# Stage ends of a two-block network on one core: residual sums in pairs, an early norm sum, one rounding pass, and an eight-slot ring for the query weights

## The chip, the core and the metric

The kernel runs on one core of a Trainium2 chip. The metric is the device time of one execution in microseconds, smaller is better. TensorE (PE in the profile) multiplies, VectorE (DVE), ScalarE (ACT) and GpSimd (POOL) do elementwise work, and DMA queues issued by SyncE (SP) and POOL bring weights from memory. All engines run their own instruction streams in order and meet in semaphores.

## The reference

One activation x of 256 tokens by 1024 features goes through ten sublayers, each of the same frame: normalise, mix, add to x.

```
h = modulate(x, norm_g, shift, scale)      # rms_norm over the 1024 features, then scale and shift
x = x + gate[:, None, :] * sublayer(h)     # (0.5 * gate for the four swiglu sublayers)
```

The sublayers in order: swiglu (0), the bidirectional SSD mixer (1), swiglu (2), swiglu (3), latent attention, MLA (4), swiglu (5), then twice an RWKV and pooling mixer (6, 8) followed by PEER (7, 9), and a last rmsnorm. PEER is

```
q = (h @ peer_q).reshape(B, S, PEER_HEADS, 2, PEER_HALF)
scores = jnp.einsum('bshpd,hpkd->bshpk', q, peer_keys)     # then top 16 of each half, and of the sums
act = jax.nn.gelu(jnp.einsum('td,ted->te', hx, u_sel), approximate=False)
return jnp.einsum('te,ted->td', gx * act, v_sel)
```

and the kernel computes it densely over all 128 x 128 experts. At the end of SSD, y is normalised in groups and projected: `rms_norm(y) @ w_out`. Everything is float32.

## The kernel before

x lies in SBUF feature-major, as eight tiles `x[:, d, :]` of 128 features by 256 tokens. Every weight matrix is cut into blocks of 128 x 1024 float32 (512 KB), and all of them stand in one `stream` in the order of use; SP issues them one after the other, each as soon as the block before it in its slot was used (semaphore `block_used`). `ring_plan` gives each block a slot: RING = 4 slots proper, and in some stages up to eight more in a large scratch tile (`arena`; MORE). CYCLES says which slots a stage goes round.

A float32 product is made from three fast products. ACT rounds a block to its high part (`split_hi`, L1126, into one of four buffers `weights_hi`, so block n waits for block n-4), DVE subtracts and leaves the low part in the slot (`split_lo`, L1613), and PE does hi x hi, hi x lo and lo x hi: 24 matmuls for a block (L506 where the output is a column of tiles, L539 where a block adds to all eight tiles of `acc`). The output projections of the RWKV mixers (L996) use plain float32.

The frame around every stage is written by hand on four engines:

- DVE, `residual`: x[:, d] += acc[:, d] * gate for d = 0..7 (L1607), each signalled with `x_upd`. Ahead of it DVE makes the low parts of the next stage's first two blocks.
- ACT, `norm_squares`: eight squares (L1109), then Sqrt and Identity of their sum (L1111, L1112). Ahead of it ACT makes the high parts of the next stage's first two or three blocks.
- PE, `norm_sum`: eight float32 matmuls with a matrix of ones (L487, 16 records in the trace).
- DVE, `normed`: reciprocal (L1587), three refinement steps (L1534 to L1536), then h (L1592); ACT adds the shift (L1118); PE starts the next stage at L518. Between its sum and L518 PE runs 16 matmuls on zeros (`open_acc`, L493), once the low parts of the first two blocks are there.

In stages 0, 2, 3, 5 (swiglu, "row blocks") and 7, 9 (PEER) the last weights are row blocks: each adds to all eight tiles of acc, so all tiles are finished by the last block. In the mixers 1, 4, 6, 8 each output block finishes one tile ("column blocks"): SSD has 16 output blocks in two passes, MLA and RWKV eight.

In MLA, POOL issues four loads in one queue once stage 3 has updated x (L2173 to L2176): the positions, w_uq, w_ukv and a table. DVE starts the angles of the rotary embedding (L1751 to L1761) when the positions have landed, ahead of the low parts of blocks 4, 5, 6 of the stage. At the end of SSD, DVE normalises y tile by tile (L1733), ACT rounds it (L1244) and DVE takes the rest (L1728); the splits of output blocks 4 to 7 stand between these tiles. In PEER, ACT copies query k out of PSUM (L1445) and then splits block k+4, and PE makes the scores (L1040).

## Time and profile before

| | |
|---|---|
| median of 3 runs | 3544.99 us (3544.09 to 3548.17) |
| the profiled execution, its own time | 3544.45 us |
| its span, first to last instruction | 3542.7 us |
| PE busy | 3363.8 us, 95% |
| DVE, ACT, POOL busy | 73%, 1609.1 us, 6% |
| mean granted TensorE clock | 0.982 |

The profile is of one execution. "Idle before" is the time an engine had nothing to do ahead of an instruction; what stands behind the arrow is what ended that time. A busy PE also contains the 16 zero matmuls at each stage's start, and time at half clock.

### The profile page before, as it was taken

The page shows a single profiled execution, that of the slowest core. Times are in us where ns is not written, and L with a number is a line of the kernel's source. Part 1 is how long each engine was busy: PE and PEld are TensorE (multiplying, and loading weights), DVE is VectorE, ACT ScalarE, POOL GpSimd, SP SyncE. Part 2 cuts the span into 40 slices and gives each one's busy share as a digit, 9 for nine tenths or more (in the row PEclk, how much of TensorE's full clock was granted, in tenths as well). Part 3 has the DMA queues.
Part 4 walks back from the last instruction along what each step waited for, and adds up shares of the span by engine and source line. Part 5 has one row for each costly group of instructions (what it writes and reads, how often), then busy time and mean ns, then how long its engine had stood idle before and what let it go on. Part 6 is the DMA issues. An engine that isn't in the chain of part 4 may idle for free.

```text
span 3542.7 us, 68786 instructions
## 1 busy us (share of the span) xinstructions
PE 3363.8 (95%) x26804; PEld 3227.9 (91%) x26804; DVE 2582.7 (73%) x4576; ACT 1609.1 (45%) x2583; POOL 198.8 (6%) x331
## 2 busy tenths in 40 slices
PE   6999989999999998999999989999899999999998
PEld 5999869999867998889999989998789999989998
DVE  7879667788736886746977757776845978767776
ACT  3456644354445435234454444444414444444444
POOL 1100001101000220200000000000300000000000
PEclk9999999999999999999999999999999999999999
DMA  9954218869622993035664466665214665456665
GB/s 366 358 196 170 78 48 326 311 254 335 215 78 107 394 354 125 31 105 190 233 205 168 164 203 228 227 227 173 72 57 158 232 222 173 166 180 228 229 227 174
DMA packets 246577, 707.44 MB, mean 200 GB/s; under 512 B 27472, under 2 KB 93008, under 8 KB 244928
## 3 DMA queue, kind: packets, MB, share of 16 engines
q1 hardware_dynamic: 212112, 571.64, 46.3%
q0 software_dynamic: 34224, 132.46, 10.0%
q8 instruction: 166, 2.72, 0.3%
q14 instruction: 75, 0.61, 0.1%
HBM read 669.40 MB, written 34.60 MB: 199 GB/s over the span
## 4 chain that ended last, share of the span: by engine, by line
PE 83%; DVE 7%; DMA 5%; ACT 3%; issue 2%; SPq 0%; ACTq 0%; DVEq 0%; POOLq 0%; POOL 0%
PE psum L506 37%; PE psum L539 27%; PE psum L1061 3%; DMA ring<-stream 3%; PE psum L883 2%; PE psum L996 1%; PE psum L634 1%; DMA arena<-mod_weights 1%; DVE ring L1613 1%; PE psum L903 1%; DVE arena L1544 1%; PE psum L518 1%; PE psum L519 1%; ACT weights_hi L1126 1%; DVE arena L1670 1%
## 5 line engine op out<-in xcount | busy, mean ns | idle before, releaser
L1126 ACT ACTIVATE weights_hi<-ring 128x1024 fp32r<-128x1024 f32 x727 | 769.0, 1058 | 1068.3 <-DMA ring<-stream 1017.7
L1613 DVE TENSOR_TENSOR ring<-ring,weights_hi 128x1024 fp32r<-128x1024 f32 x727 | 890.0, 1226 | 477.6 <-ACT weights_hi L1126 474.5
L506 PE MATMUL psum<-hh,weights_hi 128*128 128x256 f32 x4216 | 1210.6, 287 | 20.0 <-ACT arena L1339 8.5
L506 PE MATMUL psum<-h,weights_hi 128*128 128x256 f32 x4216 | 1196.6, 284 | 0.0
L506 PE MATMUL psum<-hh,ring 128*128 128x256 f32 x3104 | 881.5, 284 | 0.0
L506 PEld LDWEIGHTS psum<-hh,weights_hi 128*128 128x128 f32 x4216 | 813.1, 193 | 27.0 <-issue 11.9
L539 PE MATMUL psum<-small,weights_hi 128*128 128x256 f32 x2752 | 783.4, 285 | 39.9 <-DVE work L1648 21.6
L506 PEld LDWEIGHTS psum<-h,weights_hi 128*128 128x128 f32 x4216 | 812.9, 193 | 0.2
L539 PE MATMUL psum<-work,weights_hi 128*128 128x256 f32 x2752 | 781.6, 284 | 0.0
L539 PE MATMUL psum<-small,ring 128*128 128x256 f32 x2304 | 651.3, 283 | 0.0
L506 PEld LDWEIGHTS psum<-hh,ring 128*128 128x128 f32 x3104 | 598.0, 193 | 0.0
L539 PEld LDWEIGHTS psum<-small,weights_hi 128*128 128x128 f32 x2752 | 523.7, 190 | 42.0 <-issue 22.7
L539 PEld LDWEIGHTS psum<-work,weights_hi 128*128 128x128 f32 x2752 | 524.1, 190 | 0.0
L539 PEld LDWEIGHTS psum<-small,ring 128*128 128x128 f32 x2304 | 438.0, 190 | 0.0
L506 PE MATMUL psum<-hh,more_lo 128*128 128x256 f32 x1112 | 315.3, 284 | 0.0
L1544 DVE SCALAR_TENSOR_TENSOR arena<-arena 128x1024 f32<-128x1024 f32 x232 | 281.7, 1219 | 9.7 <-DMA arena<-mod_weights 9.6
L1613 DVE TENSOR_TENSOR more_lo<-arena,weights_hi 128x1024 fp32r<-128x1024 f32 x198 | 241.5, 1223 | 60.2 <-ACT weights_hi L1126 60.1
L1126 ACT ACTIVATE weights_hi<-arena 128x1024 fp32r<-128x1024 f32 x198 | 208.2, 1053 | 113.6 <-PE psum L506 86.2
L506 PEld LDWEIGHTS psum<-hh,more_lo 128*128 128x128 f32 x1112 | 214.1, 193 | 0.0
L2072 DVE TENSOR_SCALAR work<-kept,small 128x128 f32<-128x128 f32 x512 | 142.7, 342 | 82.6 <-PE psum L1061 77.3
L2084 DVE TENSOR_TENSOR work<-work,arena 128x256 f32<-128x256 f32 x256 | 159.5, 625 | 5.4 <-PE psum L539 5.4
L2154 POOL DMA_DIRECT2D arena<-mod_weights x208 | 109.8, 528 | 600.5 <-DVE arena L1544 597.0
(409 smaller groups left out, 3904.7 us busy)
## 6 DMA issues: line engine op xcount, KB each, us to landing
ring<-stream SPq DMA_DIRECT2D x751, 512.0 KB, 3.5
arena<-mod_weights POOLq DMA_DIRECT2D x224, 512.0 KB, 5.9
arena<-stream SPq DMA_DIRECT2D x206, 512.0 KB, 5.5
acts<-small SPq DMA_DIRECT2D x256, 128.0 KB, 2.2
work<-acts SPq DMA_DIRECT2D x256, 128.0 KB, 2.1
arena<-cond_rows POOLq DMA_DIRECT2D x3, 1024.0 KB, 9.0
arena<-w_uq POOLq DMA_DIRECT2D x1, 3072.0 KB, 10.4
arena<-constants POOLq DMA_DIRECT2D x2, 1200.0 KB, 5.7
```

What stands on the lines that cost most here:

```text
L506: mm = pe.matmul(out, lhs[:, d, :], rhs[:, d, :], start=(d == 0 and p == 0), stop=(d == DT - 1 and p == 2))
L518: pe.matmul(out, w[:, d, :], h_hi[:, d, :], start=opens and d == 0, stop=False, skip_group_check=True)
L519: pe.matmul(out, wl[:, d, :], h_hi[:, d, :], start=False, stop=False, skip_group_check=True)
L539: mm = pe.matmul(acc[:, d, :], lhs[:, d, :], rhs, start=False, stop=False, skip_group_check=True)
L883: mm = pe.matmul(PS[:, (4 * st + b) % 8, j * P:(j + 1) * P], lhs[:, c, :], rhs[:, c, :], start=True, stop=True)
L1061: mm = pe.matmul(PS[:, 4 + g % 4, j * P:(j + 1) * P], OHI[:, g % 2, j, :], OHJ[:, g % 2, j, :], start=True, stop=True)
L1126: act.activation(whi[:, NTH[n] % WS, :], raw(n), ACT.Copy).then_inc(sem["block_hi"], 1)
L1544: return dve.scalar_tensor_tensor(PRODUCT[:, m % 2, :], block, 1.0, COND[:, 0 if g < 6 else 1, :], ALU.mult, ALU.mult, accum_out=modc[:, g ...
L1613: dve.tensor_tensor(low(n), raw(n), whi[:, NTH[n] % WS, :].bitcast(F32), ALU.subtract)\
L2072: dve.tensor_scalar(OHI[:, g % 2, j, :], iota, ijg[:, 0, t:t + 1], ijg[:, 2, t:t + 1], ALU.is_equal, ALU.mult)
L2084: dve.tensor_tensor(gat[:, k % 4, :], sil[:, k % 4, :], WALL[:, :, i * 4 + k], ALU.mult).then_inc(sem["pe_gated"], 1)
L2154: pool.dma_start(MODRING[slot], mods[i * MOD_RING + (first + slot + MOD_RING)]).then_inc(mod_full[slot], 16)
```

## The change

1. **Row-block ends** (stages 0, 2, 3, 5, 7, 9). PE signals `acc_done` in the last block when tiles 0-1, 2-3 and 4-5 are finished, and `residual` waits for those instead of for the whole block. PEER's loop over value blocks gets its last round written out for that.
2. **Mixer ends** (1, 4, 6, 8). `residual` of a pair of tiles runs as soon as their blocks are through, placed between the low-part splits; the splits of the next stage's first two blocks now stand behind tiles 0-5 and behind tiles 6-7, on ACT and on DVE. PE sums the squares of tiles 0-3 ahead of the last output block and those of 4-7 behind it.
3. **Root table.** ACT runs a one-column Sqrt at each stage end ahead of the squares.
4. **SSD.** All 16 tiles of y are rounded first, then blocks 4 to 15 are split.
5. **Query ring.** PEER's 16 query blocks go round eight slots, four of them in the arena, which is free once x was updated (`ARENA_FREE`).
6. `acc_done` takes the place of the semaphore `mla_pos`: the positions now count on `mla_w` with the other three loads, and DVE waits for all four.

```
 CYCLES = {...
-          BASE["mix_in", 0]: (0, range(RING))}
+          BASE["mix_in", 0]: (0, range(RING)), **{BASE["peer_q", l]: (0, query_cycle(l)) for l in range(2)},
+          **{BASE["uv", l]: (query_cycle(l)[0], range(RING)) for l in range(2)}}
-ARENA_FREE = {BASE["ffn", f] + RING - 1: 8 * s for f, s in ((1, 2), (3, 5))}
+ARENA_FREE = {**{BASE["ffn", f] + RING - 1: 8 * s for f, s in ((1, 2), (3, 5))},
+              **{BASE["peer_q", l] + RING: 8 * (7 + 2 * l) for l in range(2)}}
+def query_cycle(l):
+    first = (BASE["peer_q", l] - BASE["mix_in", 0]) % RING
+    return (*((first + k) % RING for k in range(RING)), *SSD_CYCLE[RING:])
+BEHIND_MIXERS = (2, 5, 7, 9)
+BY_ROWS = (0, 2, 3, 5, 7, 9)
...
-            def rows_in_parts(w, wl, hi, lo):
+            def rows_in_parts(w, wl, hi, lo, last=False):
                 for d in range(DT):
                     ...
+                    if last and d in (1, 3, 5):
+                        mm.then_inc(sem["acc_done"], 1)
...
+                        if b == 1 and d == 6:
+                            norm_sum(2, 0, 4)
...
-                pe.wait_ge(sem["mla_w"], 48)
+                pe.wait_ge(sem["mla_w"], 64)
...
+                    if d == 6:
+                        norm_sum(7 + 2 * l, 0, 4)
...
-                norm_sum(s)
+                norm_sum(s, 4 if s in BEHIND_MIXERS else 0)
...
                     act.activation(YHI[:, k, :], Y[:, k, :], ACT.Copy).then_inc(sem["ssd_yhi"], 1)
-                    if k in (8, 10, 12, 14):
-                        split_hi(o0 + k // 2)
-                for n in range(8, 2 * DT):
+                for n in range(4, 2 * DT):
                     split_hi(o0 + n)
...
             for s in range(NSUB):
-                if s and s in IN_PARTS:
-                    for p in range(3 if s in EARLY else 2):
+                act.activation(eps[:, 6 + s:7 + s], eps[:, 0:1], ACT.Sqrt)
+                if s in BEHIND_MIXERS:
+                    norm_squares(s, 0, 6)
+                    split_hi(FIRST[s])
+                    norm_squares(s, 6, DT)
+                    split_hi(FIRST[s] + 1)
+                else:
+                    for p in range(0 if s == 0 else 3 if s in EARLY else 2):
                         split_hi(FIRST[s] + p)
-                norm_squares(s)
+                    norm_squares(s, 0, DT)
+                norm_root(s)
...
+            def residual(s, last, a=0, b=DT):
+                for d in range(a, b):
+                    if s in BY_ROWS and d < 6:
+                        dve.wait_ge(sem["acc_done"], 3 * BY_ROWS.index(s) + d // 2 + 1)
+                    else:
+                        ready(last(d | 1))
+                    dve.scalar_tensor_tensor(x[:, d, :], acc[:, d, :], modc[:, s, 16 + d:17 + d], x[:, d, :], ALU.mult, ALU.add)\
+                       .then_inc(sem["x_upd"], 1)
+            def residual_by_columns(s, last, a):
+                residual(s, last, a, 6)
+                split_lo(FIRST[s + 1])
+                residual(s, last, 6, DT)
+                split_lo(FIRST[s + 1] + 1)
...
-                dve.wait_ge(sem["mla_pos"], 16)
+                dve.wait_ge(sem["mla_w"], 64)
...
-            pool.dma_start(ANG[:, 0, :].bitcast(I32), pos_d[0:1, :].to_broadcast([64, T])).then_inc(sem["mla_pos"], 16)
+            pool.dma_start(ANG[:, 0, :].bitcast(I32), pos_d[0:1, :].to_broadcast([64, T])).then_inc(sem["mla_w"], 16)
```

Three places of the instruction streams are shown as they stand in the program. The first is ACT at the end of SSD, where `weights_hi` is a split, `arena<-x` are the squares and `small<-psum,eps` is the root. Before:

```order
L1126 ACTIVATE weights_hi<-ring 128x1024 [waits block_used,slot_full_0]
L1126 ACTIVATE weights_hi<-ring 128x1024 [waits block_used,slot_full_1]
L1126 ACTIVATE weights_hi<-ring 128x1024 [waits block_used,slot_full_2]
L1109 ACTIVATE arena<-x 128x256 [waits x_upd] x8
L1111 ACTIVATE small<-psum,eps 128x256 [waits norm_sum]
```

Now:

```order
L1155 ACTIVATE weights_hi<-ring 128x1024 [waits block_used,slot_full_0]
L1520 ACTIVATE eps<-eps 128x1
L1136 ACTIVATE arena<-x 128x256 [waits x_upd] x6
L1155 ACTIVATE weights_hi<-ring 128x1024 [waits block_used,slot_full_1]
L1136 ACTIVATE arena<-x 128x256 [waits x_upd] x2
L1155 ACTIVATE weights_hi<-ring 128x1024 [waits block_used,slot_full_2]
L1140 ACTIVATE small<-psum,eps 128x256 [waits norm_sum]
```

The second split of the next stage has moved from ahead of all squares to behind the last of them, ahead of the root. The second place is DVE at the end of the first RWKV mixer, where `x<-psum,modc,x` is the residual, `ring<-ring,weights_hi` a low part, and RECIPROCAL opens the norm. Before:

```order
L1960 TENSOR_TENSOR arena<-arena 128x1024 [waits rw_bg,dve_chain]
L1613 TENSOR_TENSOR ring<-ring,weights_hi 128x1024 [waits block_hi] x2
L1607 SCALAR_TENSOR_TENSOR x<-psum,modc,x 128x256 [waits block_used] x8
L1587 RECIPROCAL small<-small 128x256 [waits norm_sqrt]
L1534 SCALAR_TENSOR_TENSOR arena<-small 128x256 [waits norm_sqrt,dve_chain]
```

Now:

```order
L2010 TENSOR_TENSOR arena<-arena 128x1024 [waits rw_bg,dve_chain]
L1642 SCALAR_TENSOR_TENSOR x<-psum,modc,x 128x256 [waits block_used] x6
L1661 TENSOR_TENSOR ring<-ring,weights_hi 128x1024 [waits block_hi]
L1642 SCALAR_TENSOR_TENSOR x<-psum,modc,x 128x256 [waits block_used] x2
L1661 TENSOR_TENSOR ring<-ring,weights_hi 128x1024 [waits block_hi]
L1623 RECIPROCAL small<-small 128x256 [waits norm_sqrt]
```

Six residuals have moved ahead of both low parts, and one low part now stands between the last residual and the reciprocal. The third is PE at the same mixer end (`arena,kept` is the norm sum, `arena,ring` an output block). Before:

```order
L996 MATMUL psum<-arena,ring 128x256 [waits slot_full_0]
L996 MATMUL psum<-arena,ring 128x256 x3
L996 MATMUL psum<-arena,ring 128x256 [waits slot_full_1]
L996 MATMUL psum<-arena,ring 128x256 x3
L996 MATMUL psum<-arena,ring 128x256 [waits slot_full_1]
L996 MATMUL psum<-arena,ring 128x256 x3
L487 MATMUL psum<-arena,kept 128x256 [waits norm_sq] x8
L493 MATMUL psum<-zeros 128x512 [waits block_lo]
```

Now:

```order
L1015 MATMUL psum<-arena,ring 128x256 x3
L499 MATMUL psum<-arena,kept 128x256 [waits norm_sq] x4
L1015 MATMUL psum<-arena,ring 128x256 [waits slot_full_1]
L1015 MATMUL psum<-arena,ring 128x256 x3
L1015 MATMUL psum<-arena,ring 128x256 [waits slot_full_1]
L1015 MATMUL psum<-arena,ring 128x256 x3
L499 MATMUL psum<-arena,kept 128x256 [waits norm_sq] x4
L506 MATMUL psum<-zeros 128x512 [waits block_lo]
```

Four of the eight sum matmuls have moved ahead of the last output block.

## Rows read from the trace of the kernel before

**Rows 1.** The page, busy time, share of the span and instructions of each engine.

```profile
PE 3363.8 (95%) x26804; PEld 3227.9 (91%) x26804; DVE 2582.7 (73%) x4576; ACT 1609.1 (45%) x2583; POOL 198.8 (6%) x331
```

**Rows 2.** Timeline of PE, first swiglu's end: start us, us, engine, line, tiles, count, idle.

```profile
242.93 3.72 PE L487 MATMUL psum<-arena,kept 128*128 128x256 f32 x16 [1.02 <-ACT arena L1109]
...
251.68 0.39 PE L518 MATMUL psum<-hh,weights_hi 128*128 128x256 f32 x1 [1.58 <-ACT hh L1118]
```

**Rows 3.** Timeline of ACT at the same place.

```profile
236.19 0.42 ACT L1148 ACTIVATE small<-arena 128x256 fp32r<-128x256 f32 x1 [2.46 <-PE psum L539]
236.51 2.00 ACT L1126 ACTIVATE weights_hi<-ring 128x1024 fp32r<-128x1024 f32 x2
239.13 1.06 ACT L1126 ACTIVATE weights_hi<-ring 128x1024 fp32r<-128x1024 f32 x1 [0.62 <-PE psum L539]
242.46 3.16 ACT L1109 ACTIVATE arena<-x 128x256 f32<-128x256 f32 x8 [2.27 <-DVE x L1607]
245.64 1.28 ACT L1111 ACT_TABLE_LOAD   x1
```

**Rows 4.** Timeline of DVE at the same place.

```profile
237.59 2.36 DVE L1613 TENSOR_TENSOR ring<-ring,weights_hi 128x1024 fp32r<-128x1024 f32 x2 [0.52 <-ACT weights_hi L1126]
241.94 3.23 DVE L1607 SCALAR_TENSOR_TENSOR x<-psum,modc,x 128x256 f32<-128x256 f32 x8 [1.99 <-PE psum L539]
...
247.44 1.75 DVE L1587 RECIPROCAL small<-small 128x256 f32<-128x256 f32 x1 [1.14 <-ACT small L1111]
```

**Rows 5.** Line L1238, a one-column Sqrt: duration min/median/max ns.

```profile
L1238 ACT ACTIVATE eps<-eps x1: 202/202/202, 486.9 to 486.9; 128x1 f32<-128x1 f32 x1
```

**Rows 6.** Timeline of PE, end of the first RWKV mixer.

```profile
1534.69 24.44 PE L996 MATMUL psum<-arena,ring 128*128 128x256 f32 x112
1558.96 3.62 PE L487 MATMUL psum<-arena,kept 128*128 128x256 f32 x16
```

**Rows 7.** Timeline of DVE at the same place.

```profile
1563.12 1.75 DVE L1587 RECIPROCAL small<-small 128x256 f32<-128x256 f32 x1 [2.16 <-ACT small L1111]
```

**Rows 8.** Timeline of PE at the end of SSD.

```profile
550.70 0.28 PE L682 MATMUL psum<-more_lo,ring 128*128 128x256 f32 x1
```

**Rows 9.** Timeline of DVE at the end of SSD.

```profile
555.98 1.75 DVE L1587 RECIPROCAL small<-small 128x256 f32<-128x256 f32 x1 [2.03 <-ACT small L1111]
```

**Rows 10.** Waits of PE from 505 to 530 us: total, times, longest.

```profile
PE psum L682 <- DVE ring L1613: 4.1, 4, 2.2
```

**Rows 11.** Line L2176, issue of the last of the four MLA loads at 968.4.

```profile
DMA to landing us min/median/max: 15.4/15.4/15.4
```

**Rows 12.** Timeline of DVE in the MLA input.

```profile
979.59 0.29 DVE L1751 CAST arena<-arena 64x256 f32<-64x256 int32 x1
...
983.75 0.29 DVE L1761 TENSOR_SCALAR arena<-arena 64x256 f32<-64x256 f32 x1
986.63 1.23 DVE L1613 TENSOR_TENSOR ring<-ring,weights_hi 128x1024 fp32r<-128x1024 f32 x1 [2.59 <-ACT weights_hi L1126]
```

**Rows 13.** Timeline of PE, block 4 of the MLA input.

```profile
987.91 0.39 PE L506 MATMUL psum<-hh,weights_hi 128*128 128x256 f32 x1 [3.06 <-DVE ring L1613]
```

**Rows 14.** Timeline of PE in the queries and scores of both PEER stages.

```profile
1580.47 0.38 PE L506 MATMUL psum<-hh,weights_hi 128*128 128x256 f32 x1 [1.33 <-DVE ring L1613]
...
1616.91 7.30 PE L1040 MATMUL psum<-arena 128*128 128x128 f32 x63 [1.63 <-ACT arena L1445]
...
2671.97 0.39 PE L506 MATMUL psum<-hh,weights_hi 128*128 128x256 f32 x1 [0.82 <-DVE ring L1613]
...
2709.60 8.81 PE L1040 MATMUL psum<-arena 128*128 128x128 f32 x62 [2.82 <-ACT arena L1445]
```

**Rows 15.** Windows: length, busy time (count) of PE, PEld, DVE, ACT, POOL; clock, DMA, GB/s.

```profile
405.00:420.00 15.00, 9.21 (x50) 6.46 (x49) 4.10 (x4) 9.23 (x21) 0.00 (x0) 0.77 0.09 35
411.00:416.60 5.60, 5.06 (x21) 3.53 (x22) 1.90 (x3) 5.30 (x13) 0.00 (x0) 0.50 0.00 0
898.40:901.30 2.90, 2.87 (x13) 2.90 (x14) 0.22 (x1) 0.00 (x0) 0.53 (x1) 0.50 0.89 329
988.00:991.40 3.40, 3.40 (x29) 3.40 (x30) 2.47 (x3) 3.40 (x8) 0.00 (x0) 1.00 0.05 18
2709.60:2713.80 4.20, 4.20 (x23) 4.20 (x24) 0.93 (x1) 2.14 (x3) 0.00 (x0) 0.59 0.01 6
```

**Rows 16.** Timeline of PE where a long wait of a swiglu stage ends.

```profile
898.43 0.55 PE L539 MATMUL psum<-small,weights_hi 128*128 128x256 f32 x1 [4.25 <-DVE work L1648]
```

More of the change, by code:

```diff
@@ L290, in build @@
         zeros = sb("zeros", [P, P], BF16)
-        eps = sb("eps", [P, 6])
+        eps = sb("eps", [P, 20])
         modc = sb("modc", [P, NSUB, 24])
@@ L482, in arrived, with norm_sum @@
                 return raw(n).rearrange("p (k c) -> p k c", k=8)
-            def norm_sum(s):
-                for d in range(DT):
+            def norm_sum(s, a=0, b=DT):
+                for d in range(a, b):
                     pe.wait_ge(sem["norm_sq"], 8 * s + d + 1)
-                    mm = pe.matmul(PS[:, 2, 0:T], ones, SQ[:, d, :], start=(d == 0), stop=(d == DT - 1))
-                mm.then_inc(sem["norm_sum"], 1)
+                    mm = pe.matmul(PS[:, 2, 0:T], ones, SQ[:, d, :], start=(d == 0), stop=(d == DT - 1), skip_group_check=True)
+                if b == DT:
+                    mm.then_inc(sem["norm_sum"], 1)
             def open_acc():
@@ L1065, in peer, with value @@
                 open_acc()
-                with pe.Fori(0, NK // 4) as i:
+                def value(k, i, last=False):
+                    w, wl = parts(v0 + k, i)
+                    pe.wait_ge(sem["gate_lo"], i * 4 + (GATES["uv", l] + k + 1))
+                    rows_in_parts(w, wl, gat_hi[:, k, :], gat_lo[:, k, :], last)
+                with pe.Fori(0, NK // 4 - 1) as i:
                     for k in range(4):
-                        w, wl = parts(v0 + k, i)
-                        pe.wait_ge(sem["gate_lo"], i * 4 + (GATES["uv", l] + k + 1))
-                        rows_in_parts(w, wl, gat_hi[:, k, :], gat_lo[:, k, :])
+                        value(k, i)
+                for k in range(4):
+                    value(k, NK // 4 - 1, k == 3)
             def begin(s):
-                norm_sum(s)
+                norm_sum(s, 4 if s in BEHIND_MIXERS else 0)
             pe.wait_ge(sem["inits"], 4)
@@ L1103, in ready, with norm_squares @@
                 act.wait_ge(sem["block_used"], i * STEP + (n + 1))
-            def norm_squares(s):
-                for d in range(DT):
+            def norm_squares(s, a, b):
+                for d in range(a, b):
                     if s:
@@ L1510, in _ @@
                     peer((s - 7) // 2)
-            norm_squares(NSUB)
+            act.activation(eps[:, 6 + NSUB:7 + NSUB], eps[:, 0:1], ACT.Sqrt)
+            norm_squares(NSUB, 0, DT)
+            norm_root(NSUB)
         @block.vector
@@ L1598, in normed, with residual_by_rows @@
                     split_lo(FIRST[s] + 3)
-            def residual(s, last):
+            def residual(s, last, a=0, b=DT):
+                for d in range(a, b):
+                    if s in BY_ROWS and d < 6:
[4 more added lines that the diff above has]
+                       .then_inc(sem["x_upd"], 1)
+            def residual_by_rows(s, last):
                 if s + 1 in FIRST:
@@ L1604, in residual @@
                         split_lo(FIRST[s + 1] + p)
-                for d in range(DT):
-                    ready(last(d | 1))
-                    dve.scalar_tensor_tensor(x[:, d, :], acc[:, d, :], modc[:, s, 16 + d:17 + d], x[:, d, :], ALU.mult, ALU.add)\
-                       .then_inc(sem["x_upd"], 1)
+                residual(s, last)
+            def residual_by_columns(s, last, a):
[3 more added lines that the diff above has]
+                split_lo(FIRST[s + 1] + 1)
             def split_lo(n, i=0):
@@ L1657, in ffn @@
                     products(2 * FT + j)
-                residual(s, lambda d: base + 3 * FT - 1)
+                residual_by_rows(s, lambda d: base + 3 * FT - 1)
             def ssd():
@@ L1736, in ssd @@
                         rest_of_y(k - 1)
-                    if k in (8, 10, 12, 14):
-                        split_lo(o0 + k // 2)
                 rest_of_y(ZT - 1)
-                for n in range(8, 2 * DT):
+                for n in range(4, 2 * DT):
                     split_lo(o0 + n)
-                residual(1, lambda d: BASE["ssd_out"] + DT + d)
+                    if n in (13, 15):
+                        residual(1, lambda d: o0 + DT + d, n - 13, n - 11)
+                residual_by_columns(1, lambda d: o0 + DT + d, 4)
             def mla():
-                dve.wait_ge(sem["mla_pos"], 16)
+                dve.wait_ge(sem["mla_w"], 64)
                 c1, c2 = 6.28125, 1.93500518798828125e-3
@@ L1822, in mla @@
                     split_lo(o0 + n)
-                residual(4, lambda d: o0 + d)
+                    if n in (5, 7):
+                        residual(4, lambda d: o0 + d, n - 5, n - 3)
+                residual_by_columns(4, lambda d: o0 + d, 4)
             def rwkv(l):
@@ L2104, in peer @@
                     gate_lo(k + 2, NK // 4 - 1)
-                residual(7 + 2 * l, lambda d: BASE["uv", l] + 2 * NK - 1)
+                residual_by_rows(7 + 2 * l, lambda d: BASE["uv", l] + 2 * NK - 1)
             dve.wait_ge(sem["inits"], 4)
```

9 lines of the change are left out of this document (6 added, 3 removed).

## The prediction

> **What bounds the kernel now.** The page's row of busy times comes first: PE is busy 95% of the span, and the next engine, DVE, 73% [rows 1]. So an edit pays only where it shortens an idle time of PE or a stretch at half clock; what it takes off ACT or DVE elsewhere is worth nothing. Then the timelines of one stage end. In stage 0 the last matmul ends at E = 242.93 - 1.02 = 241.91. From there the chain runs: DVE's residuals from 241.94 (eight in 3.23, 0.40 each) [rows 4], ACT's squares from 242.46, PE's sum from 242.93 for 3.72 (it starts on the first squares and ends behind the last), a table load at 245.64 for 1.28 [rows 2, 3], the root, the reciprocal at 247.44 [rows 4], and the next stage's first matmul at 251.68 [rows 2]. That is 5.5 us from E to the reciprocal, and 4.24 from there, which the change leaves alone. The 16 zero matmuls lie in this second part, so PE looks busy in a time that is chain. Outside the ends the change touches three places where PE waits: output blocks of SSD [rows 10], block 4 of MLA [rows 13], and queries and scores of PEER [rows 14].
>
> **A. Row-block ends (minus 4.4).** The last elementwise step of the stage on ACT ends at 236.61, 5.3 ahead of E, and the splits for the next stage follow [rows 3]. Now a root table load (1.28, rows as above) and a one-column Sqrt (0.20 [rows 5]) stand between: the pair of splits (2.00) begins near E - 3.8, and DVE's pair of low parts (2.36, begun 1.1 behind the splits [rows 4]) ends near E - 0.4. The residuals can start there and not earlier, although tiles 0-1 are finished 18 matmuls before E: the splits, not PE, now set their start. Before, it was E + 0.03, so 0.48 is won. Behind the squares the load of 1.28 vanishes, but ACT's last square ended at 245.62 while PE's sum ended at 246.65; the root waited for the later of load (246.92) and sum. Without the load it waits for the sum: 0.24 won. Together 0.7 for stages 0, 2 and 5. In 3 ACT's splits wait for blocks to land and I take 0.6; in 7 both splits and low parts are late for that cause, 0.2. At stage 9 no splits follow, so residuals start as their tiles finish; the reciprocal then lies as at the RWKV end, where residuals already run during the last blocks: 1563.12 - 1559.13 = 3.99 behind E [rows 6, 7], against 5.5: 1.5. Sum 3 x 0.7 + 0.6 + 0.2 + 1.5 = 4.4. Bounds: 2 if the splits slip by what ACT now has in front of them; 9 if at each end the reciprocal came at 3.99.
>
> **B. Mixer ends (plus 2.6).** Half of PE's sum is moved ahead of the last output block: eight records of 3.62/16 = 0.226 [rows 6], taken as 1.72 for their pitch of 0.215. PE has nothing to wait for there (112 matmuls in 24.44 without a gap [rows 6]), so nothing hides it: the stage's last matmul moves to E' = E + 1.72. What follows E' is shorter: residuals of tiles 6 and 7 (0.87), their squares to E' + 1.4, then the high part of block F + 1 (1.06 [rows 3]) before the root on ACT, and the low part of F + 1 (1.23 [rows 12]) before the reciprocal on DVE, which comes at E' + 3.5 = E + 5.2. SSD had it at 555.98 - 550.98 = 5.00 [rows 8, 9]: plus 0.2. MLA's end, with its table load, I take as unchanged. The RWKV ends had 3.99: plus 1.2 each. Sum 2.6. Bounds: 0 if PE's early sum falls into a pause that the new order makes; 4 x 1.72 = 6.9 if the part behind E' is not shortened at all. Queued behind the low part of F + 1 are the reciprocal on DVE and the zero matmuls on PE, which begin near E' + 3.6 and take 3.6, ending about half a microsecond ahead of the first matmul's input: costed at nothing on that cover; a later low part would be paid in full.
>
> **C. SSD (minus 1.9).** PE waits four times, 4.1 in all, longest 2.2 [rows 10]. The longest is output block 4 landing, before any split, and stays. The other three, 1.9 together, fall where splits stand between roundings of y; all roundings are ahead now. Bounds: 0 (DVE's rest of y is the slow partner) to 1.9.
>
> **D. MLA's positions (plus 4.3).** The angles took DVE from 979.59 to 984.04, 4.45, as soon as the positions were there; then DVE idled 2.59 and made the low part of block 4 at 986.63 [rows 12]; PE began the block at 987.91 after a wait of 3.06 [rows 13]. Now DVE waits for all four loads. The last was issued at 968.4 and landed 15.4 later [rows 11]: 983.8, or some 0.3 earlier as stage 3 ends earlier. The angles then end near 988.05, the low part near 989.3, and PE starts at 989.4, where it could have started at 987.3 (part A): plus 2.0, with the idle time at 5.1. Queued behind the wait on DVE are the low parts of blocks 4, 5 and 6, and PE waits for them. The second cost is the clock. After the wait of 3.06 here the granted clock was 1.00; after 4.25 elsewhere [rows 16] the next 2.90 us ran at 0.50; in 405 to 420, where PE idled 5.8 in all, 5.60 us behind the restart ran at 0.50 (1.2 GHz of 2.4) [rows 15]. Half of such a stretch is lost, 1.45 to 2.8; a wait of 5.1 lies nearer to the longer one, and I take 2.3. Sum 4.3, bounds 0 (the loads land earlier) to 2.0 + 2.8 + 0.6 = 5.4.
>
> The Trainium skill (TensorE: Matmul & The Clock Gate, section "HAM oscillation") counts the loss as half of the whole throttled duration, the part under idle time included. The row from 405 to 420 has a clock of 0.77, so 6.9 us of it throttled, and by the page 3.4 would be lost where my reading of the row gives 2.8; the forecast by the page would be 1.1 higher, 3538.9. The row speaks for the smaller: part of the throttled time lay where PE had no work.
>
> **E. Query ring (minus 7.3).** Blocks 4 to 7 no longer wait for a slot. Stage 7: the wait of 1.33 goes. The 1.63 before the scores came from ACT, which had to split a late block before it copied the last query; without that, what stays is the copy and two handovers, some 0.48: 1.15 won. Stage 9: 0.82 goes, 2.82 becomes 0.48 (2.34) [rows 14], and with it the slow stretch behind: 4.20 at clock 0.59 [rows 15]; the scores took 8.81 for 62, at stage 7's rate of 7.30/63 it would be 7.18 [rows 14]: 1.6. Sum 2.5 + 4.8 = 7.3. Bounds: 2.6 if only the ring's own waits and a little of the others go (the keys and the new blocks share the queues), 7.9 if the score waits vanish whole. The arena slots open with the mixer's last residual, some 15 us before they are used.
>
> At nothing I cost the peeled loop round, 10 more signals, and the table load at stage 0's start (hidden: there DVE's products set the pace). If that cover were gone, 1.3 for the table.
>
> **Sum.** -4.4 + 2.6 - 1.9 + 4.3 - 7.3 = -6.7; from the profiled execution's own 3544.45 that is 3537.8. The median is 0.5 above this execution. About 0.2%, 7.1 us, is what a measurement of this kernel can tell from no change, so the forecast stands on that border.
>
> **Rivals.** (1) *MLA costs nothing*: the last load lands early enough, or the clock holds as it did after 3.06. Then -6.7 - 2.3 = -9.0 at least, 3535.4. Against it, 15.4 is a measured landing. (2) *The mixer ends lose the clock*: behind E' PE has only residual time, then four sums, then nothing till the low part of F + 1, 1.6 and 0.5 us idle, and a wait of 2.82 was enough for 0.59 [rows 14, 15] while 3.06 was not [rows 13]. If each of four ends lost the most that rows show, 2.8 or 2.9, that is 11.6: 3549.4, slower than before; it decides from 1.7 an end. Against it: the first part before E' is dense work. (3) *Landing bounds the queries*: part E gives only 2.6, 3542.5, no change. For it: weights come at 329 GB/s in a loaded stretch [rows 15], and the eight slots ask for more at once. (4) *The early signals work fully*: residuals start before the splits matter and the mixer sum is hidden; A gives 9 and B 0: -6.7 - 4.6 - 2.6 = -13.9, 3530.5.
>
> **How the numbers follow.** Forecast 0.48 (its own range 3534.5 to 3541), rival 1 0.15, rival 2 0.08, rival 3 0.13, rival 4 0.13, the rest 0.03. The range runs from 3531.0, which leaves out half of rival 4 and what is below, to 3545.0, which leaves out rival 2 and the rest. Faster by over 0.2% means under 3537.9: half of the forecast, rival 1 and most of rival 4, 0.50. Slower needs 3552.1: half of rival 2 and a bit, 0.05. The rest, 0.45, is no change that shows.
>
> **What the new profile would show.** A: reciprocal at E + 4.8 at stage 0, with the low parts ending just before the first residual, and E + 4.0 at the last end. B: sum records in two lots of eight; in the RWKV mixers the reciprocal 3.5 behind the last matmul, and that matmul 1.7 later. C: one PE wait left in the output blocks of SSD. D: an idle time near 5 ahead of MLA's block 4, and a clock of 0.5 behind it. E: no wait at query block 4, about 0.5 ahead of the scores, and 7.2 to 7.4 for the second scores. The forecast fails if the landing of MLA's loads has moved, if the low part of F + 1 delays the reciprocal, or if the ten ends drop the clock anywhere new.

## The result and the profile after

The changed kernel takes 3525.15 us, the median of 5 runs (3516.6 to 3529.28), against 3544.2 for the kernel before on the same chip (3543.79 to 3548.17). The ratio is 0.9941, with an interval of 0.9927 to 0.9956: 19 us less, where 6.7 were forecast and 3531.0 was the low end of the range. The busy times hardly differ from [rows 1]; here from the page of the changed kernel:

```profile
PE 3352.7 (95%) x26804; PEld 3213.5 (91%) x26804; DVE 2582.6 (73%) x4576; ACT 1610.4 (46%) x2594; POOL 199.4 (6%) x331
```

PE does the same 26,804 matmuls in 11.1 us less busy time. A shorter wait does not shorten busy time, so most of the gain is no wait at all. First the places that the prediction named.

The end of stage 0 in the changed kernel, timelines of PE, ACT and DVE (start, duration, engine, line):

```profile
239.85 3.72 PE L499 MATMUL psum<-arena,kept 128*128 128x256 f32 x16 [0.51 <-ACT arena L1136]
...
248.36 0.39 PE L531 MATMUL psum<-hh,weights_hi 128*128 128x256 f32 x1 [1.33 <-ACT hh L1147]
```

```profile
234.11 1.28 ACT L1520 ACT_TABLE_LOAD   x1
235.41 0.20 ACT L1520 ACTIVATE eps<-eps 128x1 f32<-128x1 f32 x1
235.52 2.94 ACT L1155 ACTIVATE weights_hi<-ring 128x1024 fp32r<-128x1024 f32 x3
```

```profile
236.59 2.36 DVE L1661 TENSOR_TENSOR ring<-ring,weights_hi 128x1024 fp32r<-128x1024 f32 x2 [2.04 <-ACT weights_hi L1155]
238.87 3.22 DVE L1642 SCALAR_TENSOR_TENSOR x<-psum,modc,x 128x256 f32<-128x256 f32 x8
...
244.11 1.75 DVE L1623 RECIPROCAL small<-small 128x256 f32<-128x256 f32 x1 [0.89 <-ACT small L1140]
```

E is 239.85 - 0.51 = 239.34. (E is the end of the stage's last matmul, as in the prediction.) The splits wait behind the table load, the residuals start 0.47 ahead of E, right behind the low parts, and the reciprocal comes 4.77 behind E instead of 5.53 [rows 2, 4]. The end of the first RWKV mixer, PE and then DVE:

```profile
1553.37 1.89 PE L499 MATMUL psum<-arena,kept 128*128 128x256 f32 x8
1555.10 3.62 PE L1015 MATMUL psum<-arena,ring 128*128 128x256 f32 x16
```

```profile
1561.06 1.23 DVE L1661 TENSOR_TENSOR ring<-ring,weights_hi 128x1024 fp32r<-128x1024 f32 x1 [1.43 <-ACT weights_hi L1155]
1562.20 1.75 DVE L1623 RECIPROCAL small<-small 128x256 f32<-128x256 f32 x1
```

Eight sum records stand ahead of the last block (1553.37 to 1555.10, 1.73), and the reciprocal comes 1562.20 - 1558.72 = 3.48 behind the last matmul, right behind the low part. The MLA input, DVE, PE, and the window behind PE's restart (length, busy time, count for PE, PEld, DVE, ACT, POOL, then clock):

```profile
976.63 0.29 DVE L1799 CAST arena<-arena 64x256 f32<-64x256 int32 x1 [4.88 <-DMA arena<-constants]
```

```profile
982.40 0.58 PE L519 MATMUL psum<-hh,weights_hi 128*128 128x256 f32 x1 [5.36 <-DVE ring L1661]
```

```profile
981.00:987.90 6.90, 5.50 (x26) 5.50 (x27) 4.72 (x5) 2.68 (x5) 0.00 (x0) 0.51 0.01 3
```

DVE now waits for the last load (arena<-constants), PE idles 5.36, and the next 5.5 us run at half clock, 2.7 us lost. Last the waits of PE in SSD's output blocks and from the second PEER's start to its scores (total, times, longest), and these scores:

```profile
PE psum L697 <- DVE ring L1661: 2.2, 1, 2.2
```

```profile
PE psum L1061 <- ACT arena L1472: 0.5, 1, 0.5
PE psum L531 <- ACT hh L1147: 0.4, 1, 0.4
```

```profile
2699.22 7.41 PE L1061 MATMUL psum<-arena 128*128 128x128 f32 x64 [0.47 <-ACT arena L1472]
```

One wait is left in SSD, none at the query blocks, 0.47 ahead of the scores, and these run at full pace.

So the steps of the forecast stand in the trace. What is new lies where PE waits for nothing. The windows below are of PE alone: 70 to 160 lies in the column blocks of stage 0, 3200 to 3400 in the row blocks of the second PEER; columns are length, busy time (count of matmuls), clock, DMA share, GB/s. Before:

```profile
70.00:160.00 90.00, 90.00 (x752) 1.00 0.97 365
3200.00:3400.00 200.00, 200.00 (x1669) 1.00 0.68 228
```

and after:

```profile
70.00:160.00 90.00, 90.00 (x752) 1.00 0.97 365
3200.00:3400.00 200.00, 200.00 (x1699) 1.00 0.70 232
```

PE is busy all the time at full clock in all four, yet fits 30 more row-block matmuls into the same 200 us. Taken over the whole trace, as the mean time from the recorded start of one matmul to the next of the same line (distances of 100 to 130 ns, which leaves waits and half clock out; this time is called the pace below), column blocks (L506, now L519) stay at 119.92 and 119.93 ns, and row blocks (L539, now L552) go from 119.99 to 118.35. With some 8,100 such distances that is 13.3 us, all four swiglu stages and both PEER stages having a part. Within one trace the row blocks change among 117.3, 118.7 and 120.0 from stretch to stretch.

### The profile page after: what moved, and what is told of

It is laid out like the page before. It is cut to its first block, busy times and chain, and to the rows that moved or that the text cites. A ratio compares the mean times of both kernels' runs of the same rounds, so it can differ in the third digit from the quotient of the medians.

```text
span 3523.1 us, 68787 instructions
## 1 busy us (share of the span) xinstructions
PE 3352.7 (95%) x26804; PEld 3213.5 (91%) x26804; DVE 2582.6 (73%) x4576; ACT 1610.4 (46%) x2594; POOL 199.4 (6%) x331
## 4 chain that ended last, share of the span: by engine, by line
PE 83%; DVE 7%; DMA 5%; ACT 2%; issue 2%; SPq 0%; POOL 0%; DVEq 0%; POOLq 0%; ACTq 0%
PE psum L519 37%; PE psum L552 26%; PE psum L1082 3%; DMA ring<-stream 2%; DMA arena<-mod_weights 2%; PE psum L902 2%; PE psum L1015 1%; PE psum L649 1%; DVE ring L1661 1%; DVE arena L1580 1%; PE psum L922 1%; PE psum L697 1%; PE psum L531 1%; ACT weights_hi L1155 1%; PE psum L532 1%
## 5 line engine op out<-in xcount | busy, mean ns | idle before, releaser
L519 PE MATMUL psum<-hh,weights_hi 128*128 128x256 f32 x4216 | 1210.7, 287 | 21.0 <-ACT arena L1366 8.4
L519 PE MATMUL psum<-h,weights_hi 128*128 128x256 f32 x4216 | 1195.8, 284 | 0.0
L1155 ACT ACTIVATE weights_hi<-ring 128x1024 fp32r<-128x1024 f32 x711 | 751.9, 1058 | 955.5 <-DMA ring<-stream 899.7
L1661 DVE TENSOR_TENSOR ring<-ring,weights_hi 128x1024 fp32r<-128x1024 f32 x711 | 870.2, 1226 | 412.1 <-ACT weights_hi L1155 407.1
L519 PE MATMUL psum<-hh,ring 128*128 128x256 f32 x2976 | 843.9, 284 | 0.0
L519 PEld LDWEIGHTS psum<-hh,weights_hi 128*128 128x128 f32 x4216 | 812.7, 193 | 27.8 <-issue 12.4
L552 PE MATMUL psum<-small,weights_hi 128*128 128x256 f32 x2752 | 780.4, 284 | 40.3 <-DVE work L1696 22.9
L519 PEld LDWEIGHTS psum<-h,weights_hi 128*128 128x128 f32 x4216 | 812.7, 193 | 0.3
L552 PE MATMUL psum<-work,weights_hi 128*128 128x256 f32 x2752 | 778.1, 283 | 0.0
L552 PE MATMUL psum<-small,ring 128*128 128x256 f32 x2304 | 649.5, 282 | 0.0
L519 PEld LDWEIGHTS psum<-hh,ring 128*128 128x128 f32 x2976 | 573.2, 193 | 0.0
L552 PEld LDWEIGHTS psum<-small,weights_hi 128*128 128x128 f32 x2752 | 525.2, 191 | 43.3 <-issue 23.9
L552 PEld LDWEIGHTS psum<-work,weights_hi 128*128 128x128 f32 x2752 | 525.3, 191 | 0.0
L552 PEld LDWEIGHTS psum<-small,ring 128*128 128x128 f32 x2304 | 438.0, 190 | 0.0
L519 PE MATMUL psum<-hh,more_lo 128*128 128x256 f32 x1240 | 351.6, 284 | 0.0
L1661 DVE TENSOR_TENSOR more_lo<-arena,weights_hi 128x1024 fp32r<-128x1024 f32 x214 | 261.1, 1223 | 76.8 <-ACT weights_hi L1155 73.7
L1155 ACT ACTIVATE weights_hi<-arena 128x1024 fp32r<-128x1024 f32 x214 | 225.0, 1053 | 114.1 <-PE psum L519 87.0
L519 PEld LDWEIGHTS psum<-hh,more_lo 128*128 128x128 f32 x1240 | 238.7, 192 | 0.0
```

The lines of the kernel that those rows point to most:

```text
L519: mm = pe.matmul(out, lhs[:, d, :], rhs[:, d, :], start=(d == 0 and p == 0), stop=(d == DT - 1 and p == 2))
L552: mm = pe.matmul(acc[:, d, :], lhs[:, d, :], rhs, start=False, stop=False, skip_group_check=True)
L1155: act.activation(whi[:, NTH[n] % WS, :], raw(n), ACT.Copy).then_inc(sem["block_hi"], 1)
L1661: dve.tensor_tensor(low(n), raw(n), whi[:, NTH[n] % WS, :].bitcast(F32), ALU.subtract)\
```

## What the diff holds beside the parts

## Experiments

**e1, e2: the place alone, and everything but the place.** The first is the kernel before with one edit:

```
-        eps = sb("eps", [P, 6])
+        eps = sb("eps", [P, 20])
```

> The kernel before with one edit: the tile eps has 20 columns and not 6, as the change made it, so that work and small, declared behind it, lie 64 bytes higher. In the changed kernel the summands of my prediction came out nearly as forecast (about 7 us), and some 12 us more were won in stretches where PE never waits: the matmuls of the row blocks follow each other every 117.3 to 118.7 ns, before every 120.0; those of the column blocks stay at 120.0. Theory P (place): the moving operands of the row blocks (in small and work) lie elsewhere, and that sets the pace. Then this kernel alone gains 8 to 14 us, 3530 to 3536, and its row blocks run at 117.3 to 118.7 ns. Rival C (code): the pace comes from the instructions that the change adds or from the peeled loop; then 3544, no difference, 120.0 ns.

Measured: 3532.23 against 3547.92, ratio 0.9955 (0.9940 to 0.9969). Row blocks 118.28 ns, column blocks 119.94. The row-block window:

```profile
3200.00:3400.00 200.00, 200.00 (x1685) 1.00 0.71 230
```

The second is the changed kernel with the old addresses:

```
-        eps = sb("eps", [P, 20])
+        sb("room", [P, 6])
...
         small, (gat_hi, _) = sb_twice("small", ...)
+        eps = sb("eps", [P, 20])
```

> The changed kernel, but eps is declared behind small and a tile of 6 columns stands in its old place, so that work and small lie at the addresses that they had before. Theory P: the row blocks go back to 120.0 ns, and the time is what my forecast's steps alone give, 3536 to 3538. Rival C: as the changed kernel, 3525, with 117.3 to 118.7 ns.

Measured: 3537.37 (3535.94 to 3545.64), ratio 0.9966 (0.9953 to 0.9979). Row blocks 119.99 ns. The reciprocals stand as in the changed kernel, 4.72 behind E at stage 0 and 3.49 and 3.48 at the mixers; only at stage 7 does it come later, 5.97 behind E instead of 5.08. Both edits answer for the place, and the rival is out: the code without the new place has the old pace, the new place without the code the new one. As a number the time is what the forecast's steps gave (3537.8), but that comes of another chip; its distance to the 3547.9 of before on that chip, 7.5 to 16.7 by the interval, is somewhat more than 6.7. Both kernels spread over some 10 us there, so e2's total is no finer test than that.

**e3: the query ring alone** (part 5 of the diff put into the kernel before).

> The kernel before with the query ring alone (part E). Forecast of that part: minus 7.3 against before, 3537: waits of 1.33 and 0.82 at query block 4 gone, the waits ahead of the scores 0.5 instead of 1.6 and 2.8, and no half clock in the second scores. Rival: the new blocks compete with the keys for the queues, minus 2.6.

Measured: 3541.99, ratio 0.9981 (0.9972 to 0.9990), 3.5 to 9.9 us less. From the first matmul of the stage to the end of its experts, stage 7 is 1.7 shorter and stage 9 5.4, 7.1 together against 7.3; up to the end of the scores, where the step was priced, it is 2.7 and 5.0. PE's waits in 2655 to 2730, where [rows 14] had 0.82 and 2.82:

```profile
PE psum L528 <- ACT hh L1128: 1.3, 1, 1.3
PE psum L1050 <- ACT arena L1455: 0.5, 1, 0.5
```

**e4: MLA's positions waited for alone.**

```
-                dve.wait_ge(sem["mla_w"], 64)
+                dve.wait_ge(sem["aux_loads"], 32)
...
-            ... to_broadcast([64, T])).then_inc(sem["mla_w"], 16)
+            ... to_broadcast([64, T])).then_inc(sem["aux_loads"], 16)
```

> The changed kernel, but the positions count on a semaphore of their own (the one of an early load), and DVE waits for them alone, as before (part D undone). Forecast of that part: 4.3 less than the changed kernel, 3521, the wait ahead of block 4 of MLA near 3 us and no half clock behind it. Rival: the clock does not follow the wait, 2.0 less; or the loads are not late, no difference. The pace of the row blocks varies from run to run in the changed kernel (3516.6 to 3529.3), so the difference is to be read in the MLA stage of the profile.

Measured: 3523.99 (3519.81 to 3528.8), ratio 0.9927 (0.9914 to 0.9939). PE's wait ahead of block 4, and the clock behind it:

```profile
981.13 0.39 PE L519 MATMUL psum<-hh,weights_hi 128*128 128x256 f32 x1 [3.27 <-DVE ring L1661]
```

```profile
981.60:985.00 3.40, 3.40 (x19) 0.50 0.02 6
```

The wait is back at 3.3, but against the expectation the clock fell here too, for 3.4 us (1.7 lost), which it had not after 3.06 in [rows 13, 15]. From the first matmul of MLA to its last the three traces have 159.7 (before), 166.1 (changed) and 163.1 (e4). Of the 6.4 between the first two 1.7 is the early sum, so the positions cost 4.7 against the trace of before, and 3.0 against e4, whose clock happened to fall.

**e5 to e8: four other places.** To e4's kernel, whose tiles lie as in the changed one: unused tiles ahead of h and ahead of modc, with eps declared last:

```
+        sb("room_h", [P, 8])      # 8, 16, 24, 32: h and hh 32, 64, 96, 128 bytes up
         h, (h_lo,) = sb_twice("h", ...)
...
-        eps = sb("eps", [P, 20])
+        sb("room", [P, 8])        # 8, 16, 16, 16: small and work 32, 96, 128, 160 bytes up
```

> The last run had moved nothing; here, in the changed kernel with its own wait for positions, unused tiles are put ahead of h and work, and eps is declared last. Addresses modulo 128: h and hh (moving operands of the column blocks) 32, before 0; small and work (of the row blocks) 0; they were 96 in the kernel before (pace 120.0 ns) and 32 in the changed one (117.3 to 118.7). Theory M (the start modulo 128 decides): the column blocks take over the pace 117.3 to 118.7 that the row blocks had at 32, and win 1 to 2% of some 1500 us, 15 to 28 us; the row blocks at 0 go back to 120.0, as the column blocks had at 0, and lose 12. Together 3507 to 3525. Rival R (where the moving operand lies relative to weights_hi, ring and the results decides): no rule by 128, paces other than these.

> As the run before, with h, hh, small and work all at 64 modulo 128. Theory M: rows and columns have one pace, whichever it is; if only 32 is good, both 120.0 ns and 3534 to 3538. Rival R: two paces.

> As the run before, all at 96 modulo 128, where the row blocks of the kernel before stood (128 bytes below). Theory M: both at 120.0 ns, 3534 to 3538. Rival R: the rows differ from 120.0 although the remainder is the same.

> As the run before, with h and hh 128 bytes above their old place, so at 0 modulo 128 as before; small and work at 0. Theory M: both at 120.0 ns, 3534 to 3538, the columns as before because the remainder is the same. Rival R: a pace other than 120.0 in the column blocks, since the absolute place is new.

Measured: 3504.24 (ratio 0.9873, 0.9854 to 0.9891), 3475.49 (0.9793, 0.9777 to 0.9809), 3524.89 (0.9931, 0.9915 to 0.9948) and 3528.11 (0.9939, 0.9922 to 0.9955). The windows of e6:

```profile
70.00:160.00 90.00, 90.00 (x766) 1.00 0.98 373
3200.00:3400.00 200.00, 199.43 (x1704) 1.00 0.72 232
```

The column blocks can be moved to a better pace too, and they are the larger family. Theory M fell: at 96 modulo 128 the rows had 119.99 before and 118.32 in e7, and rows and columns at 64 have two paces, 115.34 and 117.38. The guess that only 32 is good gave 3534 to 3538 for e6; it was the best of the four.

**e9, e10: everything moved, or hh without h.** An unused tile of 64 bytes ahead of ring (e9) or between h and hh (e10), in the kernel before.

> The kernel before with one edit: an unused tile of 64 bytes ahead of ring, so that every tile, weights and moving operands alike, lies 64 bytes higher. So far the mean distance of two matmuls was, with h at +0, 32, 64, 96, 128 bytes: 119.92, 116.86, 117.38, 119.92, 119.05 ns; with small and work at +0, 32, 64, 96, 128, 160: 119.99, 118.95, 118.35, 115.34, 118.32, 119.98. The remainder by 128 alone does not give these, but 32 and 64 are the fast ones. Theory D (distance between the moving operand and the weights decides, the two being read side by side): both paces stay at 119.9 and 120.0 ns and the time at that of before. Rival A (the absolute address decides): columns 117.4, rows 118.4, and 30 to 50 us less than before.

> The kernel before with an unused tile of 64 bytes between h and hh: the low part h stays where it was, the high part hh and what lies behind (small and work too) are 64 bytes higher. hh is read by two of three matmuls of a column block, h by one. If each moving operand acts by itself, the columns get two thirds of the gain at +64, from 119.9 to some 118.2 ns; if both must be in the same place, they stay at 119.9 or become slower. Rows 118.4 as in the changed kernel at +64.

Measured: e9 3550.13, ratio 1.0006 (0.9995 to 1.0017), 119.91 and 119.98 ns; e10 3530.38, ratio 0.9951 (0.9935 to 0.9968), columns 118.90, rows 118.10. The stage 0 window of e9 has the old count:

```profile
70.00:160.00 90.00, 90.00 (x753) 1.00 0.97 365
```

Absolute addresses are out. In e10 columns won 1.0 ns, against 2.5 with both parts moved: less than the two thirds expected, and more than nothing. The single steps show more. The two of three that start with a matmul on hh take 117.3 ns in the mean, the pace of a column block at +64, and the one that starts with h takes 122.0, more than the 119.9 that it had before. So each operand shows its own place, and h beside a moved hh is worse off than both in the old place.

**e11, e12: the norm sum whole, and another pair of places.** e11 is e6 without `norm_sum(s, 0, 4)` ahead of the last output blocks; e12 is e6 with h at +32.

```
-                    if d == 6:
-                        norm_sum(7 + 2 * l, 0, 4)
...
-                norm_sum(s, 4 if s in BEHIND_MIXERS else 0)
+                norm_sum(s)
```

> The layout of e6 (h and work at 64 modulo 128) with a part of the change undone: PE makes the whole norm sum behind the last output block of the four mixers (DVE and ACT keep the new order). By part B of the prediction the early half costs 1.72 us of PE and is not won back: the last matmul comes 1.7 earlier and the reciprocal 4.0 behind it instead of 3.5, so 1.2 less at each of four ends, 4.8 less than e6. Rival: without the early half the sum cannot start before the squares of tiles 6 and 7, and the reciprocal comes 5.2 behind the last matmul, no difference.

> Each family at its best place so far: h and hh at +32 bytes (116.86 ns), small and work at +96 (115.34 ns). If a family's pace hangs on its own place alone, the columns are 0.5 ns faster than in e6, 12,200 x 0.5 = 6 us less than e6. Rival: the small difference between +32 and +64 is one of runs, not of place, and the time equals e6's within 5 us.

Measured: e11 3479.54 (ratio 0.9803, 0.9787 to 0.9819), e12 3486.98 (0.9831, 0.9809 to 0.9853), columns 117.58 and 117.06 ns, rows 116.22 and 115.64. The reciprocal of e11 comes 4.00 behind the last matmul at all four mixers, as forecast, but the paces differ from run to run by more than 4.8 us makes. e12 was expected 6 below e6 and won nothing on it, by ratio either (0.9831 against 0.9793).

**e13, e14: what the distance is taken from, and its period.** In the kernel before, an unused tile of 64 bytes behind weights_hi (e13), or of 256 bytes ahead of h (e14).

> The kernel before with an unused tile of 64 bytes behind weights_hi: ring and weights_hi keep their place, everything else (arena, x, h, hh, small, work) lies 64 bytes higher, the distances among it unchanged. Theory W (what counts is the distance from the moving operand to the weights that are loaded beside it): columns near 117.4 ns as in e6, rows near 118.1 to 118.4 as in the changed kernel and e10; blocks whose low part lies in the arena, moved along, gain less. About 40 us less than before. Rival O (distance to other tiles, where the other engines and DMA work): 119.9 and 120.0 ns, no difference.

> The kernel before with an unused tile of 256 bytes ahead of h, so that h, hh, small and work lie 256 bytes higher. By +128 the columns went from 119.92 to 119.05 ns and the rows from 119.99 to 118.32. If the pace repeats every 256 bytes: 119.9 and 120.0 ns, no difference. Rival: it doesn't, and the paces come out like those at +128, 10 to 20 us less.

Measured: e13 3512.22, ratio 0.9904 (0.9887 to 0.9920), by it 34 us less, where about 40 were expected; columns 117.30 ns, rows 118.45. e14 3550.28, ratio 1.0006 (0.9995 to 1.0017), 119.92 and 119.99. Their windows of stage 0, e13 first:

```profile
70.00:160.00 90.00, 90.00 (x776) 1.00 0.99 379
```

```profile
70.00:160.00 90.00, 90.00 (x753) 1.00 0.99 367
```

e13 and e9 differ only in whether ring and weights_hi moved along. The output blocks of SSD and MLA, whose moving operands lie in the arena, went from 119.8 to 120.0 in the other traces to 117.5 and 117.8 in this one. So the distance to ring and weights_hi counts, and 256 bytes more change nothing. ACT, DVE and the DMA write these two as well, a rival to the weights that PE reads there. It does not fit: the column steps of e13 take 117.31 ns with DVE busy and 117.25 without, 117.36 and 117.24 with ACT busy and not, 117.24 and 117.58 with more than two DMA packets under way and fewer; in the trace before all six lie at 119.9 to 120.0. Sorted by the distance from weights_hi to the moving operand modulo 256, one remainder gives nearly one mean in all traces so far, within 0.6 ns, and within 0.9 for the rows at 192 (worked out as above):

```
remainder  mean distance of matmuls, ns
   0       columns 119.92 (before), 119.91 (e9), 119.92 (e14); rows 119.98 (e8)
  32       columns 116.86 (e5), 117.06 (e12)
  64       columns 117.38 (e6), 117.58 (e11), 117.30 (e13)
  96       rows 119.99 (before, e2, e3, e14), 119.98 (e9); columns 119.92 (e7)
 128       rows 118.95 (e5); columns 119.05 (e8)
 160       rows 118.35 (changed), 118.28 (e1), 118.64 (e4), 118.45 (e13), 118.10 (e10)
 192       rows 115.34 (e6), 116.22 (e11), 115.64 (e12)
 224       rows 118.32 (e7)
```

**e15, e16: a place that the curve names.** Columns had not been at 192; `room_h` and `room` get 48 columns each.

> The changed kernel with its own wait for positions; h and hh 192 bytes above their old place, small and work at 192 modulo 256 from weights_hi as in e6. Theory W256 (the remainder of the distance by 256 decides, for both families): columns 115.3 to 116.2 ns, as the rows had there, against 117.4 in e6; 12,200 x 1.2 to 2.1 = 15 to 25 us less than e6, 3450 to 3462. Rival: the rows' 115.3 belongs to the row blocks, and the columns stay above 117.

> As e15, with PE's norm sum whole behind the last output block of the four mixers, as in e11. By part B 4.8 us less than e15, the last matmul of a mixer 1.7 earlier and the reciprocal 4.0 behind it instead of 3.5. e11 against e6 showed 4.0 and 3.49 in the profile, but the two times could not be told apart.

Measured: e15 3455.80 (3454.34 to 3459.72), ratio 0.9731 (0.9718 to 0.9745); columns 114.04 ns, rows 116.18. e16 3456.22 (3446.04 to 3464.9), ratio 0.9739 (0.9725 to 0.9752); 113.81 and 115.25. The page of e15 and its two windows:

```profile
PE 3270.5 (95%) x26804; PEld 3125.1 (90%) x26804; DVE 2583.7 (75%) x4576; ACT 1609.0 (47%) x2594; POOL 196.6 (6%) x331
```

```profile
70.00:160.00 90.00, 90.00 (x767) 1.00 0.98 370
3200.00:3400.00 200.00, 199.72 (x1718) 1.00 0.73 235
```

The time fell into the range that the rule gave (3450 to 3462), but the columns, expected at 115.3 to 116.2, were faster than the rows at that place. The window of stage 0 in e16, which has the same layout:

```profile
70.00:160.00 90.00, 90.00 (x797) 1.00 1.01 390
```

The same blocks at the same place make 767 matmuls in one trace and 797 in the other. Taken block by block, the means above are mixtures. At remainders 64 and 192 alike a block runs either at some 113.4 ns or at some 117.8 and at nothing between, and the remainders differ in how often: of the column blocks 5 to 11% are at the fast level at 64 (e6, e11, e13) and 87 to 91% at 192 (e15, e16), of the row blocks 36 to 58% at 192 (e6, e11, e12, e15, e16). No trace has a block at the fast level at another remainder.

The end of the first RWKV mixer in e16, PE and DVE:

```profile
1519.38 3.62 PE L501 MATMUL psum<-arena,kept 128*128 128x256 f32 x16
```

```profile
1523.54 1.75 DVE L1619 RECIPROCAL small<-small 128x256 f32<-128x256 f32 x1 [0.43 <-ACT small L1136]
```

That is 4.00 behind E = 1519.54, and without the 1.73 ahead of it. The two medians do not show the 4.8 us; only the stage end in the profile does.

## Why the prediction was wrong

The step that failed is the sentence on what is costed at nothing. It names the peeled loop, the signals and a table load, and not the wider eps, and the whole sum takes the pace of a dense matmul as given. The tile was read as storage; what it moved was worth 13.3 us in the trace (8,100 x 1.64 ns), twice all the forecast's steps, and 16 (11 to 21) by the ratio of e1, which has that edit alone. No rival had that mechanism, so the range ended 6 us too early.

The steps themselves, each with its size from the traces:

- **A** (4.4 forecast): the way from E to the reciprocal went from 5.53 to 4.78 at stages 0, 2 and 5, to 4.93 at 3, from 6.24 to 5.08 at 7, and from 5.5 to 4.0 at the last end: 5.5. The splits set the residuals' start, as argued. Stage 7 was taken at 0.2 and shows 1.2, which is luck: its residuals stand behind low parts of blocks that land late, and how late varies. With the old order the reciprocal stands 5.5 behind E in the other traces (e1, e3, e9, e10, e13, e14) and 6.24 in the one that the prediction read; with the new order 5.08 in the changed kernel, 5.2 to 6.4 in e2, e5, e7, e8, e11 and e12, and 7.8 to 8.0 in e4, e6, e15 and e16. In those four PE's sum there takes 5.41 us instead of 3.72 at a granted clock of 0.68 to 0.72 (0.68 from 2425.3 to 2430.6 in e4). So the new order gains nothing sure at this end and loses over 2 us in some executions.
- **B** (plus 2.6): at the four mixers the last matmul is 1.7 later and the reciprocal 3.5 behind it. Before it was 5.00, 5.31 and twice 4.00 behind: 0.2, -0.1, 1.2 and 1.2, so 2.5. e11 and e16 turn it back in the profile; in the totals it is too small to be seen. Rival 2, a loss of clock there, did not occur at a mixer's end; it did at the end of stage 7, as said under A.
- **C** (minus 1.9): 4.1 of waits became 2.2.
- **D** (plus 4.3): 4.7, with a wait of 5.36 and 2.7 of clock instead of 5.1 and 2.3. The Trainium skill (TensorE: Matmul & The Clock Gate, section "HAM oscillation") counts half of the whole slow stretch, which from 6.8 us makes an estimate of 3.4 for the clock; the row of 981.0 to 987.9 gives half of 5.5, so here the measurement is the smaller, since part of the slow stretch lay under the wait. For the same reason the 2.8 of the prediction's bound is too high: of 411.0 to 416.6 PE worked in 5.06 [rows 15], which makes 2.5.
- **E** (minus 7.3): 7.1 in e3.

Together that is -5.5 + 2.5 - 1.9 + 4.7 - 7.1 = -7.3, and with the pace -20.6; the spans differ by 3542.7 - 3523.1 = 19.6. The 1 us between them is not traced, and it is a net of larger parts: PE's waits in stage 5, which no step names, rise from 15.2 to 17.8, and in stage 0 they fall from 37.7 to 36.5 and a stretch at half clock is 3.4 us instead of 6.8. That the sum of the steps comes within 1 us is therefore in part luck.

Why the pace hangs on the distance is not shown. In these traces the weight load of the next matmul is recorded beside each matmul; that the two reads get into each other's way in SBUF was the idea behind e9 and e13, and it is argued. Taken by steps, e13 does not support it in this form. In its column blocks whose low part lies in the arena, at remainder 0 where ring and weights_hi are at 64, the step beside the load from the arena takes 117.3 ns, and the slow one, 120.6, is the next, which starts with the matmul on those weights beside a load from weights_hi. Recorded starts need not be the times of the reads, so which reads meet stays open. The Trainium skill (TensorE: Matmul & The Clock Gate, section "Step-by-step: what each phase is for") says that loading the next weights doesn't take read bandwidth from the running matmul, since the two have ports of their own. That sentence gives no reason for e13 and e9 to differ; they have 117.30 and 119.91 ns, so for these float32r operands the place of the weights counts. Whether the load takes read bandwidth, or the place acts in another way, no run here shows. Also open is what makes the pace step between levels within a trace with nothing else changed, as between 117.3, 118.7 and 120.0 in the rows of the changed kernel, and why at 192 columns are more often at 113.4 ns than rows.
